# Two transformer layers' attention: the query rotation cut in two, output products of the sparse chunks first, high parts moved in ScalarE's order, attention rows scaled head by head

## What is computed

```python
for l in range(2):
    h = rmsnorm(x, g_mix[l]); cq, ckv, kr, aq, ak, av, qi, ki, wi, rq, rk, rv, rg = split(h @ w_in[l])
    q = (rmsnorm(cq, g_q[l]) @ w_uq[l]).reshape(B, S, 8, 64 + 32)     # 8 heads, 64 plain + 32 rotated
    q_rope = apply_rope(q[..., 64:]); kv = (rmsnorm(ckv, g_kv[l]) @ w_ukv[l]).reshape(B, S, 8, 128)
    o_a = mla_attention(q_nope, q_rope, k_nope, k_rope, v)      # causal softmax, p @ v
    o_b = dsa_attention(...)                                    # softmax over the 64 best keys, 4 heads
    o_c = silu(rg) * head_groupnorm(retention(...))             # 4 heads
    x = x + concatenate([o_a, o_b, o_c]) @ w_out[l]
    x = x + square(relu(rmsnorm(x, g_mlp[l]) @ w_ff1[l])) @ w_ff2[l]
```

## Time and profile before

| what | value |
|---|---|
| median of 3 runs | 1395.91 us (1393.72 to 1396.88) |
| the profiled execution's own time | 1395.43 us |
| its span, first to last instruction | 1393.4 us |
| TensorE busy | 97% of the span |
| VectorE, ScalarE, GpSimd busy | 45%, 39%, 32% |
| granted TensorE clock, mean | 0.998 of full speed |

### The profile page before, as it was taken

One profiled execution on the slowest core, in us unless ns is written; L12 is line 12 of the kernel. 1 busy time (PEld: TensorE's weight loads), 2 busy tenths in 40 slices (PEclk: granted clock), 3 DMA queues, 4 the chain that ended last, 5 costly groups with the idle time before them and its releaser, 6 DMA issues.

```text
span 1393.4 us, 19892 instructions
## 1 busy us (share of the span) xinstructions
PE 1347.1 (97%) x7754; PEld 931.0 (67%) x7754; DVE 622.7 (45%) x1060; ACT 541.0 (39%) x790; POOL 449.3 (32%) x295
## 2 busy tenths in 40 slices
PE   8998999999999999999999999999999999999998
PEld 7786788887887788888887877755434444344343
DVE  5685554544687455353344887523202112122021
ACT  6667644435576654343555562212111111111011
POOL 2384454444374544543867913000000000000000
PEclk9999999999999999999999999999999999999999
DMA  7441454553533355455786351479999999999997
GB/s 289 137 168 67 152 181 181 185 202 127 207 116 110 116 204 190 181 182 181 237 278 225 103 208 52 137 290 411 422 428 428 427 428 428 428 427 427 428 423 292
DMA packets 50250, 351.99 MB, mean 253 GB/s; under 512 B 7747, under 2 KB 9679, under 8 KB 25583
## 3 DMA queue, kind: packets, MB, share of 16 engines
q1 hardware_dynamic: 49438, 349.52, 64.9%
q10 hardware_dynamic: 720, 1.20, 0.2%
HBM read 347.78 MB, written 1.07 MB: 250 GB/s over the span
## 4 chain that ended last, share of the span: by engine, by line
PE 72%; DMA 11%; DVE 7%; ACT 3%; issue 3%; DVEq 2%; POOL 1%; SPq 0%; ACTq 0%; POOLq 0%
PE psum L1925 12%; PE psum L1101 9%; PE psum L1103 9%; PE psum L1102 9%; PE psum L1396 9%; DMA ring<-in_w_expert_up 8%; PE psum L1946 5%; PE psum L1398 4%; PE psum L1091 4%; PE psum L1853 2%; POOL weights_split L908 1%; PE psum L1863 1%; DMA arena<-in_w_expert_down 1%; DVE arena L2577 1%; ACT weights_split L2040 1%
## 5 line engine op out<-in xcount | busy, mean ns | idle before, releaser
L908 POOL TENSOR_TENSOR weights_split<-weights_raw,weights_split 128x512 fp32r<-128x512 f32 (+2 forms) x253 | 401.6, 1621 | 338.2 <-ACT weights_split L2040 338.2
L2040 ACT ACTIVATE weights_split<-weights_raw 128x2048 fp32r<-128x2048 f32 (+4 forms) x154 | 243.5, 1586 | 243.5 <-PE psum L1103 145.3
L1925 PE MATMUL psum<-ring,arena 128*64 128x512 f32 x944 | 226.5, 598 | 12.1 <-DMA ring<-in_w_expert_up 11.2
L1396 PE MATMUL psum<-h_split,weights_split 128*128 128x512 f32 x512 | 182.1, 399 | 3.1 <-DVE h_split L2028 2.7
L1925 PEld LDWEIGHTS psum<-ring,arena 128*64 128x64 f32 x944 | 73.4, 138 | 136.4 <-issue 135.8
L1101 PE MATMUL psum<-weights_split,h_split 128*128 128x512 f32 (+3 forms) x400 | 151.9, 380 | 4.3 <-POOL weights_split L908 2.4
L1101 PE MATMUL psum<-weights_split,hidden_split 128*128 128x512 f32 (+1 forms) x384 | 151.1, 393 | 4.3 <-DVE hidden_split L2028 4.3
L908 DVE TENSOR_TENSOR weights_split<-weights_raw,weights_split 128x2048 fp32r<-128x2048 f32 (+3 forms) x53 | 119.3, 2257 | 70.1 <-ACT weights_split L2040 68.3
L1102 PE MATMUL psum<-weights_split,h_split 128*128 128x512 f32 (+3 forms) x400 | 149.5, 374 | 0.0
L1103 PE MATMUL psum<-weights_split,h_split 128*128 128x512 f32 (+3 forms) x400 | 149.2, 373 | 0.0
L1103 PE MATMUL psum<-weights_split,hidden_split 128*128 128x512 f32 (+1 forms) x384 | 147.3, 384 | 0.0
(11 more groups left out here) (379 smaller groups left out, 1734.5 us busy)
## 6 DMA issues: line engine op xcount, KB each, us to landing
weights_raw<-in_layer_w SPq DMA_DIRECT2D x94, 1024.0 KB, 4.8
arena<-in_w_expert_down SPq DMA_DIRECT2D x28, 2048.0 KB, 14.7
ring<-in_w_expert_up SPq DMA_DIRECT2D x28, 2048.0 KB, 15.0
ring<-in_w_expert_gate SPq DMA_DIRECT2D x23, 2048.0 KB, 16.2
weights_raw<-in_second_w SPq DMA_DIRECT2D x44, 512.0 KB, 4.7
arena<-in_w_expert_gate SPq DMA_DIRECT2D x4, 2048.0 KB, 10.2
ring<-in_w_expert_up SPq DMA_DIRECT2D x8, 1024.0 KB, 13.1
arena<-in_w_expert_down SPq DMA_DIRECT2D x16, 512.0 KB, 12.3
```

Of the source, the lines that this page charges most:

```text
L908: ins = eng.tensor_tensor(W.part(j, 1, n)[:, cols], W.raw(j, n)[:, cols], W.part(j, 0, n).bitcast(F32)[:, cols], ALU.subtract)
L1396: pe.matmul(both.rearrange("p (w s) -> p w s", w=2), w[0][:, k, f * P:(f + 1) * P], hTp[:, :, k, :], start=(k == 0), stop=False)
L1925: ins = pe.matmul(bank[half(j), :], xe[h][:, k, half(j)], w[j][:, k, :], start=(k == 0), stop=(k == KD - 1))
L2040: act.activation(W.part(j, 0, w), W.raw(j, w), ACT.Copy).then_inc(W.hi, 1)
```

## The change

It edits the layers' attention in six places, in the order of four engines and of the plan.

- VectorE: `rotate_queries(c)` turns four heads at a time; the first half stands right after `norm_probs(1)`, ahead of the work on the retention results, the second right after `norm_probs(3)`, ahead of `low_values(0)`.
- VectorE: `norm_probs` scales each head by its own instruction with a scalar per partition.
- ScalarE: the high parts of out(1,1) and out(0,0) are made earlier, and `exponentials(9)` stands ahead of `empty_turned(8)`.
- TensorE: the first output products take chunks 4 and 5 of both token tiles first, then 6 and 7; they wait for the retention chunk between the two.
- TensorE: for columns 1, token tile 0, two of four products stay ahead of `attend_values(7)` (before, all four stood behind it) and two go behind the last ones of columns 0; all four of token tile 1 go behind the transposes `tr3` 0 and 1.
- The plan and `add_out(2)` follow.

```diff
@@ layer_plan @@
-    plan += [wout[0], turned[8], values[7], wout[2], turned[9], values[8], values[9], wout[1]] + turned_x[:2] + [wout[3]] + turned_x[2:]
+    plan += [wout[0], turned[8], values[7], turned[9], values[8], values[9], wout[1], wout[2]] + turned_x[:2] + [wout[3]] + turned_x[2:]
@@ TensorE @@
                 turn_retained()
-                units.wait_emptied(("O", 0), ("mixT", 3))
-                project_out(0, 1, 0, range(4))
+                units.wait_emptied(("O", 0))
+                project_out(0, 1, 0, (0, 1))
                 units.wait_emptied(("O", 2))
-                project_out(0, 1, 1, range(4), True)
+                project_out(0, 1, 1, (0, 1))
+                units.wait_emptied(("mixT", 3))
+                project_out(0, 1, 0, (2, 3))
+                project_out(0, 1, 1, (2, 3), True)
...
                 turn_probs(8)
+                project_out(1, 0, 0, (0, 1))
                 attend_values(7)
-                project_out(1, 0, 0, range(4))
                 turn_probs(9)
...
                 project_out(0, 0, 1, (3,))
-                project_out(1, 0, 1, (0, 1))
+                project_out(1, 0, 0, (2, 3))
                 units.wait_emptied(("wout", 0), ("wout", 1))
                 transposes(pe, units, "tr3", x, (0, 1))
-                project_out(1, 0, 1, (2, 3))
+                project_out(1, 0, 1, range(4))
@@ ScalarE @@
                 empty_q(1)
+                split_after("uq", 0, 2)
                 exponentials(2)
...
+                split_after("ukv", 0, 0)
                 high_values(2)
...
-                split_after("uq", 0, 2)
                 mix_gain = lambda k: gain(G_RET)(k - (KD - 2)) if k >= KD - 2 else None
                 high_transposed(act, units, "mixT", mix_gain, hTq, hT_hi, (3,))
...
                 empty_turned(4)
-                split_after("ukv", 0, 0)
                 empty_turned(5)
...
+                exponentials(9)
                 empty_turned(8)
-                exponentials(9)
@@ VectorE @@
-                    rows = scores[g % 2][:, 0:n * nk].rearrange("p (h k) -> p h k", h=n)
-                    dve.tensor_tensor(rows, rows, rinv[g % 3][:, 0:n].unsqueeze(2).to_broadcast([P, n, nk]), ALU.mult).then_inc(probs_normed.sem, 1)
+                    for j in range(n):
+                        rows = scores[g % 2][:, j * nk:(j + 1) * nk]
+                        ins = dve.tensor_scalar(rows, rows, rinv[g % 3][:, j:j + 1], None, ALU.mult)
+                    ins.then_inc(probs_normed.sem, 1)
+
+                def rotate_queries(c):
+                    units.wait_emptied(("uq", T * c), ("uq", T * c + 1))
+                    return rotate(dve, *halves(q[:, :, 4 * c:4 * c + 4, NOPE:QK]), *angles(ROPE), q_tmp)
...
                 norm_probs(1)
+                rotate_queries(0)
...
                 norm_probs(3)
+                rotate_queries(1).then_inc(q_roped.sem, 1)
                 low_values(0)
-                units.wait_emptied(*(("uq", j) for j in range(2 * T)))
-                rotate(dve, *halves(q[:, :, :, NOPE:QK]), *angles(ROPE), q_tmp).then_inc(q_roped.sem, 1)
...
-                add_out(2)
                 low_values(8)
                 low_values(9)
                 add_out(1)
+                add_out(2)
```

## The result

The changed kernel takes **1405.84 us** (median of 4 runs, 1402.53 to 1408.14) against 1396.18 us (4 runs, 1393.72 to 1396.88): a ratio of **1.0071**, 95% interval 1.0044 to 1.0097. It is slower by 0.7%, about 9.7 us, where the prediction had 1398.6 us and a range to 1404. The profiled execution took 1404.18 us (span 1402.1), 8.75 us more than that of before.

A forecast was written before the change was run, and what follows sets the result against it. TensorE, busy 97% of the span, was taken as the bound. Terms 4.0 - 1.3 + 1.3 - 2.2 - 1.2 + 0.3 + 0.7 gave +1.6 us a layer, +3.2 in all: 1398.6 us, range 1389.5 to 1404.

The forecast's parts named there:

- (b): First half of the rotation on VectorE: steps wait for GpSimd, TensorE starts the scores 4.0 us late (1.4 to 4.3).
- (h): Group 9 and the feed-forward's start: turn_probs(9) waits 1.4 us without the products ahead of it; +0.7 us (0.3 to 1.6).
- (g): Scaling of group 7 beside a busy GpSimd: two instructions wait twice, +0.3 us a layer (0 to 1.1).
- (d): Keys and retention: new waits of 0.7 us at the key transposes and 0.6 at turn_retained, +1.3 us (0 to 2.5).
- (e): First output products: chunks 4 and 5 first remove the 2.17 us wait for the retention chunk, -2.2 us a layer.
- (c): Second half of the rotation, behind norm_probs(3): the 1.33 us wait ahead of the query transposes goes, -1.3 us a layer.
- (f): Transposes of group 6: the 1.20 us wait for the scaling falls, -1.2 us a layer; it may keep some.
- (a): Scaling by head, groups 0 and 1: turn_probs(1) starts about 1.3 us late; the term vanishes in (b).
- pairs pass GpSimd together: Rival on VectorE beside GpSimd, or the locks are short: (b) 1.4 to 2.6 us, total 1389.4 to 1391.8 us; chance 0.23.
- the loss is not won back on ScalarE: Rival: ScalarE carries 4.5 us on to groups 4 to 6; +4.4 us a layer, 1404 us; chance 0.12.
- The moves did not cancel: Denies the rival that TensorE's waits only change places: within 1 us a layer, 1394 to 1397 us; chance 0.20.
- the tie at the scores: attend_scores(2, 3) starts right behind VectorE's second subtraction, which empties bank 7 at 100.22 us; work ahead of it delays TensorE.

The follow-up runs named there:

- half-covered kernel: The changed kernel with its two early triples of columns 1 (six products) behind attend_values(7) instead of ahead of it: 1402.08 us, ratio 1.0031.
- the tail: The kernel before with only the later output products in the new order, with the edits to the plan, exponentials(9) and add_out(2): 1401.41 us, 1.0036.
- the sparse chunks: The kernel before with only the first output products in the new order, chunks 4 and 5 of both tiles, then 6 and 7: 1392.62 us, 0.9959.
- three small moves: The kernel before with chunks 4 and 5 first, the whole rotation ahead of low_values(0), out(0,0)'s high part right behind exponentials(5): 1388.74 us, 0.9948.
- the tail undone: The changed kernel with the later output products (columns 1), the plan, add_out(2) and exponentials(9) as before: 1402.41 us, 1.0041.

## Why the prediction was wrong

**The step that failed is (b), in how it counted the wait.** It said that TensorE starts the scores 4.0 us late and put 4.0 into the sum. The start was 3.53 us late, so the cause and its size were right. But the sum took a wait at its length alone. Behind the 2.39 us that TensorE waits the granted clock is 0.50, and 7.43 us of work take 9.03: +1.60 a layer, as much as the whole forecast for a layer. No stretch of the attention showed a fall in the profile of before; a wait of 2.17 us there had left the clock at 1.00, and the prediction gave the longer one no price and no place in the range. Filling the wait brought the clock back to 1.00 and the scores to 1.13 us, which shows the cause. This term alone carries 3.2 of the 5.5 us by which the profiled difference exceeds the forecast.

**(h) was taken too low.** Its wait lay at the upper bound: 1.4 us forecast, up to 1.3 more for a second GpSimd step, 2.61 measured, since the scaling ends with GpSimd's low part. At the transposes of group 8 the delay is 2.31 us (144.48 for 142.17), so (g) was 0.35 for 0.3 and (h) 1.29 for 0.7 in the first layer, inside its bounds. The second layer adds 1.5 us for the clock behind that wait, which no term has.

**(d) and (e)** together gave -0.75 for -0.9. The two new waits of (d) are 0.40 and 0.84 us, forecast 0.7 and 0.6. (e) alone gives back 0.71 of its 2.17 at group 4, which in the changed kernel shows as 0.20 at group 5.

**Right:** (c), where the rotation ended at 111.9 (forecast 112.2) and the wait went, with the clock held too; the steps of (b) on VectorE, first half over at 101.6 (forecast 101.9); GpSimd's low part at 103.9 (104.2); (f), the wait at group 6 gone; and that (a) vanishes in (b), which the kernel with the whole scaling bears out more strongly than was thought: the rotation is tied to GpSimd's end and to the copies of the queries.

**The rivals.** That pairs pass GpSimd together is refuted by three rotation steps in a row of 1.22 to 1.36 us. That the loss is not won back on ScalarE is refuted as a mechanism: group 6 does not wait. The moves did not cancel. The range's upper end, 1404, was that rival's price; with a fall of the clock at one place in each layer (3.2 us) it would have reached 1407.

What stays open: why the clock fell behind 2.61 us in one layer and not in the other, and behind 2.02 but not behind 2.01 or, in the profile of before, 2.17; and how much of the 9.7 us between the medians is the change's, as a half-covered kernel that gains nothing in the rows of its first layer stands at 1.0031. The parts do not add up either: the tail (+0.36%), the high parts (+0.29%), the scaling (+0.44%) and the sparse chunks (-0.41%) leave nearly nothing over for a rotation that by the kernel with it undone costs 0.2 to 0.3%.

## What to carry to other kernels

A wait on TensorE can cost more than its length: of a change that lengthens one or puts two short ones together, ask what the clock does behind it, and add the slower matmuls to the bad end of the range. A VectorE instruction with two SBUF inputs that moves beside GpSimd's work can end with GpSimd's step and not after its own duration, so such a move is priced by GpSimd's timeline; splitting it into smaller ones can multiply that wait (scaling by head alone: 0.44% slower). And try the parts of a bundle alone: here one of them carried all of the gain, and three small moves that keep clear of the tie at the scores beat both kernels.

## What the hardware showed that was not expected

- The granted clock fell to 0.50 behind waits of 2.4 us at the scores in every profiled layer that has them (the changed kernel, the tail undone, the half-covered one: six of six) and cost 1.6 us each; so it did behind 2.4 us at the query transposes and at the first output products (the high parts alone, four of four). Behind longer waits at `turn_probs(9)`, 2.6 to 2.75 us, it fell in seven layers of ten. So the length of a wait does not decide it alone.
- One profile's scaling, unchanged in start and form, took 1.74 us instead of 0.79 when GpSimd's steps had begun 0.26 us earlier. In the second block a VectorE instruction took 4.29 us for 2.06 in the same way and TensorE waited 3.4 us behind it, in kernels that do not touch that block.
- Scaling by a scalar per head is hardly quicker by itself. Two instructions of 128x256 took 0.62 us beside an idle GpSimd (at 109.75 us in the changed kernel), where the one broadcast multiplication of 128x512 took 0.69 (at 104.41 us before). The Trainium skill's page "VectorE: DVE Perf Modes" (section "Mode 2×_2P") gives such an f32 form two elements a cycle; the 0.07 us between the two rows is what was left of it here.
